# Two attention and scan layers on one core: another order of VectorE and ScalarE work around TensorE

## The chip, the cores and the metric

The kernel runs on one core of a Trainium2 chip, in one launch. The metric is the device time of that core in microseconds (us). The engines are TensorE (PE in the rows; its weight loads are PEld), VectorE (DVE), ScalarE (ACT), GpSimd (POOL) and SyncE (SP), which here only issues the loads of weight tiles. Each engine works through its own program in order; engines wait for each other by semaphores.

## The reference

All tensors are float32. A first block (two layers with feed-forward parts, a pooling mixer and a dilated attention, 512 tokens of width 1024) gives `x`. A second block runs two more layers, and the change lies in these alone. Cut to what matters, one of them is

```python
h  = x  * (1 + scale)   + shift          # 512 latent tokens
hc = cx * (1 + scale_c) + shift_c        # 256 context tokens
(a_q, a_i, a_ff, a_fb, b_q, b_k, b_v, c_q, c_k, c_v, d_q, d_k, d_v, g_lat) = split(h @ w_in)
y_a = hgrn2(a_q, a_i, a_ff, a_fb, ...)                # gated linear scan, forward and backward
y_b = global_gqa(rope(rms(b_q)), rope(rms(b_k)), b_v) # softmax attention, latents and context
y_c = rms(diff_attention(rope(c_q), rope(c_k), c_v, lam))
y_d = window_gqa(rope(d_q), rope(d_k), d_v, sink)     # |i - j| <= 128, plus context, plus a sink
y   = concat(y_a, y_b, y_c, y_d) * silu(g_lat)
x   = layer_norm(alpha * x + gate * (y @ w_out))
```

The scan takes `f = lb + (1 - lb) * sigmoid(z)` as its forget gate, and sums of `log f` over 128 tokens, in both directions. The first of the two layers computes the context's outputs too; the second needs the 512 latents alone.

## The kernel before, in words

**Projections.** A weight tile (1024 x 128) is loaded, rounded by ScalarE to a high part (`hi`, L944), the rest is taken by GpSimd (`remainder`, L843), and TensorE multiplies high and low parts in three passes (`mm3`, L1320). In the two mixer layers a tile is cut into four *quarters* of two 128-row chunks each, so that other work fits between them. Behind the last quarter VectorE takes the result from PSUM (`fill_take`), and a `finish` step ends what the tile needs: head norm, transposed values (L1763, then a copy on VectorE, L2422), rotation (`fill_end`, L2440 to L2444). ScalarE's step behind a quarter of part 3 rounds the tile after the next and, for gates, runs a Silu between two table loads.

**Attention.** There are six attentions a layer (global, diff, window, two head pairs each). For attention `a`, `scores` (TensorE, L1788) are computed in units; VectorE copies each from PSUM and takes its row maximum (L2473), ScalarE exponentiates and sums it (L1227). When all units are done, `rows` makes one number a row out of maxima and sums: a chain of small steps between VectorE (L2495 to L2513) and ScalarE (L1237, L1239), then TensorE transposes (L1799) and ScalarE copies the row (L1241). Then come groups of keys: `weights` (TensorE, L1815) are the transposed scores with the row's number added, ScalarE exponentiates them (L1250), `values` (L1836) sums them into the output. `scores` of attention `a + 1` and `weights` of attention `a` share PSUM banks 2 and 3, so each waits until the other's banks have been read. `end` scales the output by the gate (L2525; diff attentions have a norm first: ScalarE's square L1258, TensorE's L1846, ScalarE's L1261) and splits it in a high and a low part (L1937, L1938).

**The scan.** Per head pair and direction, `sums` makes the sums of log f from the projected gate: a softplus on ScalarE (`nsp`, L989 and L990; two of them in the second layer), VectorE's steps L2314 to L2342 with six scans (L2330), and an Exp on ScalarE (L1154) that waits until VectorE has given `sums_ready`. Then six chunks go through `dist` (GpSimd), `decay` (ScalarE), `operands` (VectorE, L2267 and L2270), `products` (TensorE, L1681), `take` (VectorE, L2281 to L2289), `step` (TensorE, L1698) and `update` (VectorE).

**What sets the order.** `mixer_steps(layer)` writes one list of steps by hand, and every engine walks through it and does what it has in a step. Quarters, score units and groups are dealt out evenly; scan steps are queued in `ticks` and taken one at a time by `tick()`. In the list before the change `rows` stands for all of the chain, and `sums` has three stages: 0 (first softplus' input), 1 (its use, and the second softplus' input), 2 (all that is left, and the Exp).

## Time and profile before

| | us |
|---|---|
| median of 3 runs (lowest, highest) | 3629.45 (3626.37, 3630.61) |
| the profiled execution's own time | 3632.27 |
| its span, first to last instruction | 3630.3 |
| TensorE busy | 3244.4 |
| VectorE, ScalarE, GpSimd busy | 1747.4, 1146.8, 1216.3 |

TensorE works in most of the span; its matmuls are pipelined and their ends are modelled, so busy is not the same as at its peak. The first block lasts to about 2160 us; the first mixer layer and what ends it lie in 2160 to 2960 us, the second in 2960 to 3630 us. The clock granted to TensorE has two levels here, 1.2 and 2.4 GHz, and rows give its mean as a share of the higher.

### The profile page before, as it was taken

The page shows a single profiled execution, that of the slowest core. Times are in us where ns is not written, and L with a number is a line of the kernel's source. Part 1 is how long each engine was busy: PE and PEld are TensorE (multiplying, and loading weights), DVE is VectorE, ACT ScalarE, POOL GpSimd, SP SyncE. Part 2 cuts the span into 40 slices and gives each one's busy share as a digit, 9 for nine tenths or more (in the row PEclk, how much of TensorE's full clock was granted, in tenths as well). Part 3 has the DMA queues.
Part 4 walks back from the last instruction along what each step waited for, and adds up shares of the span by engine and source line. Part 5 has one row for each costly group of instructions (what it writes and reads, how often), then busy time and mean ns, then how long its engine had stood idle before and what let it go on. Part 6 is the DMA issues. An engine that isn't in the chain of part 4 may idle for free.

```text
span 3630.3 us, 53848 instructions
## 1 busy us (share of the span) xinstructions
PE 3244.4 (89%) x20644; PEld 2434.3 (67%) x20644; DVE 1747.4 (48%) x3135; ACT 1146.8 (32%) x1963; POOL 1216.3 (34%) x998
## 2 busy tenths in 40 slices
PE   7999889999899998998899988788979878688787
PEld 5888668777678776776678766555756655455454
DVE  4343765334634364444524366553653266554534
ACT  3222333212422132112312233443434234444343
POOL 3444444444344432222344444311331233213211
PEclk9999999999999999999999989988989988898889
DMA  3222222433233321111233321000101111001011
GB/s 134 93 98 97 77 82 82 139 122 110 100 126 107 133 81 64 53 59 47 81 133 110 122 105 36 25 19 24 36 14 64 47 53 36 30 25 36 24 53 41
DMA packets 74356, 264.66 MB, mean 73 GB/s; under 512 B 7856, under 2 KB 9136, under 8 KB 73904
## 3 DMA queue, kind: packets, MB, share of 16 engines
q1 hardware_dynamic: 67104, 242.25, 19.4%
q10 hardware_dynamic: 7056, 19.69, 1.5%
q8 instruction: 137, 2.24, 0.3%
q14 instruction: 59, 0.48, 0.0%
HBM read 252.47 MB, written 7.34 MB: 72 GB/s over the span
## 4 chain that ended last, share of the span: by engine, by line
PE 71%; DVE 15%; issue 7%; ACT 4%; POOL 2%; DMA 0%; ACTq 0%; DVEq 0%; POOLq 0%
PE ps L1320 53%; PE ps L1815 2%; PE ps L1836 2%; PE ps L1788 2%; POOL wl L855 1%; PE ps L1398 1%; DVE work L2071 1%; DVE tb L2473 1%; PE ps L1681 1%; DVE tb L2118 1%; PE ps L1623 1%; PE ps L1379 1%; PE ps L1641 1%; DVE hc L1984 1%; PE ps L1701 1%
## 5 line engine op out<-in xcount | busy, mean ns | idle before, releaser
L855 POOL TENSOR_TENSOR wl<-raw,wh 128x1024 fp32r<-128x1024 f32 x320 | 791.8, 2474 | 1220.6 <-ACT wh L966 705.4
L1320 PE MATMUL ps<-xh,wh 128*128 128x512 f32 x2400 | 916.2, 406 | 97.5 <-POOL wl L843 30.9
L1320 PE MATMUL ps<-xl,wh 128*128 128x512 f32 x2400 | 864.5, 385 | 0.0
L1320 PE MATMUL ps<-xh,wl 128*128 128x512 f32 x2400 | 862.8, 384 | 0.0
L1320 PEld LDWEIGHTS ps<-xh,wh 128*128 128x128 f32 x2400 | 442.8, 196 | 277.9 <-issue 155.5
L966 ACT ACTIVATE wh<-raw 128x1024 fp32r<-128x1024 f32 x224 | 237.6, 1061 | 982.4 <-PE ps L1320 934.0
L843 POOL TENSOR_TENSOR wl<-raw,wh 128x1024 fp32r<-128x1024 f32 x90 | 220.3, 2448 | 918.0 <-ACT wh L944 918.0
L1320 PEld LDWEIGHTS ps<-xl,wh 128*128 128x128 f32 x2400 | 443.1, 196 | 93.3 <-issue 13.1
L1320 PEld LDWEIGHTS ps<-xh,wl 128*128 128x128 f32 x2400 | 441.2, 195 | 87.6
L1320 PE MATMUL ps<-ah,wh 128*128 128x512 f32 x1104 | 437.5, 403 | 25.4 <-issue 14.2
L1320 PE MATMUL ps<-al,wh 128*128 128x512 f32 x1104 | 420.5, 388 | 0.0
L1320 PE MATMUL ps<-ah,wl 128*128 128x512 f32 x1104 | 420.3, 388 | 0.0
L944 ACT ACTIVATE wh<-raw 128x1024 fp32r<-128x1024 f32 x186 | 196.4, 1057 | 546.9 <-PE ps L1320 496.7
L1227 ACT ACTIVATE tb<-tb,work 128x256 f32<-128x256 f32 (+2 forms) x288 | 165.8, 576 | 385.0 <-DVE work L2479 185.8
L1320 PEld LDWEIGHTS ps<-ah,wh 128*128 128x128 f32 x1104 | 205.6, 189 | 106.6 <-issue 51.2
L2473 DVE TENSOR_SCALAR_CACHE_REDUCE tb<-ps 128x256 f32<-128x256 f32 (+2 forms) x288 | 135.3, 518 | 262.1 <-PE ps L1788 192.8
L2071 DVE TENSOR_TENSOR work<-work 128x512 f32<-128x512 f32 x88 | 245.2, 2786 | 0.0
L1320 PEld LDWEIGHTS ps<-ah,wl 128*128 128x128 f32 x1104 | 205.4, 189 | 43.1
L1320 PEld LDWEIGHTS ps<-al,wh 128*128 128x128 f32 x1104 | 206.0, 190 | 40.2 <-issue 2.0
L2067 DVE TENSOR_TENSOR work<-ps,rs 128x512 f32<-128x512 f32 x66 | 45.7, 692 | 300.2 <-PE ps L1320 300.1
L876 POOL TENSOR_TENSOR hc<-hc 128x64 f32<-128x64 f32 x280 | 95.7, 342 | 169.2 <-PE ps L1686 145.1
L1836 PE MATMUL ps<-work 128*64 128x512 f32 (+2 forms) x448 | 124.3, 636 | 21.0 <-issue 14.1
(348 smaller groups left out, 3625.3 us busy)
## 6 DMA issues: line engine op xcount, KB each, us to landing
raw<-wts_dram SPq DMA_DIRECT2D x458, 512.0 KB, 3.4
spilled_dram<-hc ACTq DMA_DIRECT2D x1, 3072.0 KB, 8.7
hc<-spilled_dram ACTq DMA_DIRECT2D x1, 3072.0 KB, 12.8
tb<-tab_dram ACTq DMA_DIRECT2D x5, 512.0 KB, 3.7
hc<-x_dram ACTq DMA_DIRECT2D x8, 256.0 KB, 9.2
spilled_dram<-hc ACTq DMA_DIRECT2D x1, 2048.0 KB, 7.2
hc<-spilled_dram ACTq DMA_DIRECT2D x1, 2048.0 KB, 9.3
out_dram<-hc SPq DMA_DIRECT2D x8, 256.0 KB, 2.1
```

The costliest lines, as they stand in the source:

```text
L843: pool.tensor_tensor(wl[:, n % SPLIT, :], raw[:, LOADED[n] % RAW, :], wh[:, n % SPLIT, :].bitcast(F32), ALU.subtract).then_inc(lo_done, 1)
L855: pool.tensor_tensor(wl[:, n % SPLIT, :], raw[:, LOADED[n] % RAW, :], wh[:, n % SPLIT, :].bitcast(F32), ALU.subtract).then_inc(lo_done, 1)
L876: pool.tensor_tensor(z[way], border, k_, ALU.subtract)
L944: act.activation(wh[:, n % SPLIT, :], raw[:, at % RAW, :], ACT.Copy).then_inc(hi_done, 1)
L966: act.activation(wh[:, n % SPLIT, :], raw[:, at % RAW, :], ACT.Copy).then_inc(hi_done, 1)
L1227: ins = act.activation(b, b, ACT.Exp, bias=m[:, lane, t:t + 1], scale=scale, accum_out=d[:, lane, t:t + 1])
L1320: ins = pe.matmul(out_, w[:, s, k * P:(k + 1) * P], x_(k, at), start=first, stop=last)
L1788: ins = pe.matmul(ps[:, score_bank(a) + lane, col_:col_ + n], x_[r0:r0 + w, q_tile * P:(q_tile + 1) * P], y_[r0:r0 + w, tok:tok + n], star ...
L1815: ins = pe.matmul(outs[lane], stat, mov, start=number == 0, stop=number == 3 and not g["masks"], skip_group_check=True)
L1836: pe.matmul(flat[HEAD * h:HEAD * (h + 1), g["q0"]:g["q0"] + g["n"]], vv, pring[t % len(pring)][:, 0:g["n"]], start=g["first"], stop=g["las ...
L2071: dve.tensor_tensor(tt[:, j, :], tt[:, j, :], sil[:, j, :], ALU.mult).then_inc(dve_own, 1)
L2473: ins = dve.tensor_scalar(scores_copy[:, lane, col_:col_ + n], ps[:, score_bank(a) + lane, col_:col_ + n], 1.0, -3e38, ALU.mult, ALU.max, ...
```

## The change

No instruction's work changes; what changes is where steps stand in the list, and with it the order in each engine's program.

- `sums` has the stages `abs`, `logs`, `more` (second layer), `scan`, `rest` (backward direction), `keys` and `exp`. The last is ScalarE's Exp, in a step of its own at least one step behind `keys`. `extra_tick` takes sum steps at more places.
- `rows` is split. `math` is the chain on VectorE and ScalarE and stands close behind the last score unit; `rows` is left with the transposes and the copy of the row, behind the last `values`.
- `end` no longer splits the output; `y` does, behind the first `values` of the next attention. `square` (diff) stands behind the last `values`.
- `round` is ScalarE's and GpSimd's rounding with what follows it on ScalarE (Silu, head square). In the groups it stands behind the next `weights`.
- `rope` is the rotation, split from `finish`. `table_in`, VectorE's wait for the rotation tables, stands ahead of the last quarter of the tile that needs it, no longer ahead of the first.
- In a group with several score units the first now stands ahead of the first quarter, and the first `weights` of the next attention stands behind the tail quarter.
- The diff attentions' scaled values get a semaphore of their own (`nlv_ready`).

```diff
@@ def scan_ticks
-        ticks += [[("sums", w, stage)] for stage in range(3)]
+        long = [["scan"], ["rest", "keys"]] if way else [["scan", "keys"]]
+        stages = [["abs"], ["logs"], *([["more"]] if layer else []), *long, ["exp"]]
+        ticks += [[("sums", w, stage) for stage in together] for together in stages]
+        ticks[-2].append(("dist", w, 0))
...
@@ def mixer_steps
     def scores(a, u):
+        if u == 0:
+            flush(ropes)
         steps.extend([("scores", a, u), ("exps", a, u)])
+        if a and u == units[a] - 1:
+            maths.append(("math", a))
+        flush(ropes)
...
-    def quarter(f, part):
+    def quarter(f, part, later=False):
...
         steps.append(("quarter", f, part))
+        if part == 3:
+            rounds.append(("round", f))
+            if not later:
+                flush(rounds)
...
     def finishes():
-        steps.extend(ends)
+        if ends:
+            flush(rounds)
+        for _, f in ends:
+            steps.append(("finish", f))
+            if f[0] in "qk":
+                ropes.append(("rope", f))
...
+    def extra_tick():
+        if ticks and ticks[0][0][0] == "sums":
+            tick()
...
         for i in range(n):
+            if i == 0:
+                finishes()
             if i + 1 < n:
                 steps.append(("weights", a, i + 1))
+            flush(rounds)
             finishes()
+            flush(maths)
             if i == n - 1 and not last:
                 for q in fill[i]:
                     quarter(*q)
                 finishes()
-                steps.append(("rows", a + 1))
                 fill[i] = []
             steps.append(("values", a, i))
+            if i == n - 1:
+                steps.append(("square", a))
+            if i == 0 and a:
+                steps.append(("y", a - 1))
+            extra_tick()
+            if len(due[i]) > 1:
+                scores(a + 1, due[i].pop(0))
...
+                    quarter(*step, later=True)
                 else:
+                    flush(maths)
                     tick()
+                    flush(ropes)
...
+        flush(ropes)
+        if not last:
+            steps.append(("rows", a + 1))
         if a in (1, 3):
             finishes()
             tick(len(ticks))
+        quarter(*tail, later=True)
         if not last:
             steps.append(("weights", a + 1, 0))
-        quarter(*tail)
+        flush(rounds)
         steps.append(("end", a))
...
@@ ScalarE, def sums
-                else:
+                elif stage == "exp":
                     act.wait_ge(sums_ready, w + 1)
...
@@ ScalarE, def mixers
+                def square_(a):
+                    if ATTENDS[a][0] == "diff":
+                        n_q = out_tiles(layer) * P
+                        act.wait_ge(v_used, c.at("item"))
+                        act.activation(osq[:, 0:n_q], banks(0, n_q), ACT.Square).then_inc(osq_ready, 1)
...
@@ VectorE, def mixers
+                def mixed(a):
+                    kind, hp = ATTENDS[a]
+                    n_q = out_tiles(layer) * P
+                    t = sg2[:, 0:n_q]
                     y = 2 * ["scan", "global", "diff", "window"].index(kind) + hp
                     split(t, ahk(y, TOK)[:, 0:n_q], alk(y, TOK)[:, 0:n_q], a_ready, "a")
```

Three places show how this moves instructions. Line numbers are those of each kernel, so a step has another number behind the change.

The first is on ScalarE in the second mixer layer, at the backward sums of the first head pair. Before: the rounding of a tile, a Silu between two table loads, the exponentials of a score unit, the second softplus, the load of the tables, the sums' Exp (L1154), the exponentials of a group's weights (L1250).

```order
L944 ACTIVATE wh<-raw 128x1024
L1198 ACT_TABLE_LOAD
L1198 ACTIVATE hc<-hc 128x512
L971 ACT_TABLE_LOAD
L1227 ACTIVATE tb,work<-tb,work 128x256 x4
L989 ACTIVATE hc<-hc 128x768
L990 ACTIVATE hc<-hc,sm 128x768
L1218 DMA tb<-tab_dram 128x1024
L1154 ACTIVATE work<-work,sm 128x768
L1250 ACTIVATE work<-ps 128x512 x2
```

Behind the change the same stretch reads:

```order
L1277 ACTIVATE tb,work<-tb,work 128x256 x4
L1045 ACTIVATE hc<-hc 128x768
L1046 ACTIVATE hc<-hc,sm 128x768
L1268 DMA tb<-tab_dram 128x1024
L1303 ACTIVATE work<-ps 128x512 x2
L1000 ACTIVATE wh<-raw 128x1024
L1248 ACT_TABLE_LOAD
L1248 ACTIVATE hc<-hc 128x512
L1027 ACT_TABLE_LOAD
L1277 ACTIVATE tb,work<-tb,work 128x512 x2
L1206 ACTIVATE work<-work,sm 128x768
```

The weights' exponentials (now L1303) have passed the rounding, the Silu and the sums' Exp (now L1206), which stands behind one more score unit; the two softplus pairs are still ahead of them.

The second is on TensorE in the first mixer layer, at the sixth group of the second attention. Before: a score unit (L1788), the group's weights (L1815) and values (L1836), then the next quarter (L1320).

```order
L1788 MATMUL ps<-ex,ah 128x256 x4
L1788 MATMUL ps<-ex,al 128x256 x2
L1815 MATMUL ps<-ex,ah 128x512 x2
L1815 MATMUL ps<-ex,al 128x512 x2
L1815 MATMUL ps<-ex,ah 128x512 x2
L1815 MATMUL ps<-lrow,ones_r 128x512 x2
L1836 MATMUL ps<-work 64x512 x2
L1320 MATMUL ps<-xh,wh 128x512
```

Behind the change (scores L1845, quarter L1377, weights L1872, values L1895):

```order
L1845 MATMUL ps<-ex,ah 128x256 x4
L1845 MATMUL ps<-ex,al 128x256 x2
L1377 MATMUL ps<-xh,wh 128x512
...
L1377 MATMUL ps<-xh,wl 128x256
L1872 MATMUL ps<-ex,ah 128x512 x2
L1872 MATMUL ps<-ex,al 128x512 x2
L1872 MATMUL ps<-ex,ah 128x512 x2
L1872 MATMUL ps<-lrow,ones_r 128x512 x2
L1895 MATMUL ps<-work 64x512 x2
```

A whole quarter of twelve matmuls now stands between the last score unit and the weights that use the same banks.

The third is on VectorE in the first mixer layer, ahead of the fourth attention. Before: the rotation of key tile k4 (L2440 to L2444), then the chain of the row statistics (L2495 to L2513).

```order
L2440 TENSOR_TENSOR work<-work,tb 128x512
L2441 TENSOR_TENSOR work<-work 128x512
L2442 CAST ex<-work 128x512
L2444 TENSOR_TENSOR ex<-work,ex 128x512
L2495 TENSOR_TENSOR work<-work 128x16
L2502 TENSOR_TENSOR work<-work 128x16
L2503 TENSOR_TENSOR work<-work 128x16
L2507 TENSOR_TENSOR work<-work 128x24
L2508 TENSOR_SCALAR work<-work 128x24
L2509 CAST hcol<-work 128x24
L2512 COPY work<-hcol 128x24
L2513 TENSOR_TENSOR work<-work,hcol 128x24
```

Behind the change:

```order
L2560 TENSOR_TENSOR work<-work 128x16
L2567 TENSOR_TENSOR work<-work 128x16
L2568 TENSOR_TENSOR work<-work 128x16
L2572 TENSOR_TENSOR work<-work 128x24
L2573 TENSOR_SCALAR work<-work 128x24
L2574 CAST hcol<-work 128x24
L2577 COPY work<-hcol 128x24
L2578 TENSOR_TENSOR work<-work,hcol 128x24
L2470 CAST ex<-ps 128x256
L2471 TENSOR_TENSOR ex<-ps,ex 128x256
L2472 STREAM_SHUFFLE work<-ps 128x512
L2473 TENSOR_TENSOR work<-ps,tb 128x512
```

The chain now stands ahead of the rotation and of the take of k4 from PSUM (L2470 to L2473) as well.

## Rows read from the trace of the kernel before

**Rows 1.** Busy us by engine, granted clock, DMA, in the two mixer layers.

```profile
2160.00:2960.00 800.00, 672.64 (x6534) 482.31 (x6534) 409.32 (x1146) 313.66 (x692) 210.18 (x385) 0.91 0.10 37
2960.00:3600.00 640.00, 520.70 (x4502) 349.50 (x4501) 326.75 (x902) 260.52 (x569) 160.12 (x264) 0.88 0.11 37
```

**Rows 2.** TensorE's waits, 2160 to 3600 us: total us, times, longest.

```profile
PE ps L1788 <- ACT work L1250: 39.2, 13, 15.7
PE ps L1799 <- DVE work L2513: 30.8, 10, 8.8
PE ps L1698 <- DVE work L2289: 24.0, 17, 6.9
...
PE ps L1815 <- issue: 17.6, 9, 4.9
PE ps L1836 <- issue: 14.1, 6, 3.7
...
PE ps L1681 <- DVE hc L2270: 11.8, 11, 2.2
PE ps L1815 <- ACT work L1250: 9.9, 5, 5.4
...
PE ps L1846 <- ACT work L1258: 8.9, 4, 3.3
PE ps L1763 <- DVEq L2526: 8.6, 6, 2.0
```

**Rows 3.** The chain that ended last: two quarters of twelve matmuls (start, us).

```profile
2264.81 3.62 PE ps L1320 x12
2290.77 2.30 PE ps L1320 x12
```

**Rows 4.** Timeline, second layer's backward sums: start, us, engine, line [idle before <-releaser].

```profile
3112.77 0.96 DVE L2325 SCALAR_TENSOR_TENSOR hc<-hc 128x768 f32<-128x768 f32 x1 [4.59 <-DMA tb<-tab_dram]
...
3120.26 0.93 ACT L1154 ACTIVATE work<-work,sm 128x768 f32<-128x768 f32 x1 [10.24 <-DVEq L2344]
3121.10 1.06 ACT L1250 ACTIVATE work<-ps 128x512 f32<-128x512 f32 x2
3122.21 0.80 PE L1788 MATMUL ps<-ah,ex 64*128 64x512 f32 x2 [15.70 <-ACT work L1250]
```

**Rows 5.** Timeline of TensorE: scores behind weights' exponentials that a Silu delays.

```profile
3420.75 0.80 PE L1788 MATMUL ps<-ex,ah 64*128 64x256 f32 x4 [5.96 <-ACT work L1250]
```

**Rows 6.** Timeline of TensorE at the group of the second order excerpt.

```profile
2426.93 0.28 PE L1788 MATMUL ps<-ex,al 32*128 32x256 f32 x2
2432.09 0.80 PE L1815 MATMUL ps<-ex,ah 64*128 64x512 f32 x2 [4.87 <-issue]
```

**Rows 7.** Timeline of VectorE: first and last step of one chain of row statistics.

```profile
2469.14 0.18 DVE L2495 TENSOR_TENSOR work<-work 128x16 f32<-128x16 f32 x1
...
2472.89 0.19 DVE L2513 TENSOR_TENSOR work<-work,hcol 128x24 f32<-128x24 f32 x1
```

**Rows 8.** Timeline of VectorE: the split at the end of the second attention.

```profile
2484.19 1.63 DVE L1937 CAST ah<-work 128x768 fp32r<-128x768 f32 x1
2485.85 0.96 DVE L1938 TENSOR_TENSOR al<-work,ah 128x768 fp32r<-128x768 f32 x1
```

**Rows 9.** Timelines at the second layer's start: take of q0, end of sums, head norm.

```profile
2990.60 0.68 DVE L2405 COPY work<-ps 128x512 f32<-128x512 f32 x1
...
3000.12 0.17 DVE L2342 MEMSET hc<- 128x128 f32 x1
...
2994.14 2.05 PE L1769 MATMUL ps<-work,cn 128*128 128x512 f32 x2 [5.42 <-ACT work L1169]
```

**Rows 10.** Timelines: one rotation's cast, alone and beside GpSimd's remainder.

```profile
2384.33 0.43 DVE L2442 CAST ex<-work 128x512 fp32r<-128x512 f32 x1
...
2729.55 2.91 POOL L843 TENSOR_TENSOR wl<-raw,wh 128x1024 fp32r<-128x1024 f32 x1 [27.35 <-ACT wh L944]
2730.24 2.50 DVE L2442 CAST ex<-work 128x512 fp32r<-128x512 f32 x1
```

More of the change, by code:

```diff
@@ L380, in mixer_steps, with flush @@
 def mixer_steps(layer):
-    steps, ends, ticks = [], [], []
+    steps, ends, ropes, rounds, maths, ticks = [], [], [], [], [], []
     def scores(a, u):
+        if u == 0:
+            flush(ropes)
         steps.extend([("scores", a, u), ("exps", a, u)])
-    def quarter(f, part):
-        while f[0] == "g" and f[1] in SCANS and part == 3 and ("sums", 4 * layer + 2 * SCANS.index(f[1]) + 1, 0) not in steps:
+        if a and u == units[a] - 1:
+            maths.append(("math", a))
+        flush(ropes)
+    def flush(what):
+        steps.extend(what)
+        what.clear()
+    def quarter(f, part, later=False):
+        while f[0] == "g" and f[1] in SCANS and part == 3 and ("sums", 4 * layer + 2 * SCANS.index(f[1]) + 1, "abs") not in steps:
             finishes()
@@ L432, in mixer_steps @@
         finishes()
+        if number == 0:
+            steps.append(("math", 0))
         tick()
+        flush(ropes)
     steps.append(("rows", 0))
@@ L479, in mixer_steps @@
     finishes()
+    steps.append(("y", len(ATTENDS) - 1))
     return steps
@@ L883, in mixers @@
                         dist(*at)
-                    elif step == "quarter" and at[1] == 3:
+                    elif step == "round":
                         remainder(c.at("tile"))
@@ L1239, in rows @@
                     act.activation(lnd[:, 0:n_i * n_l], den2[:, 0:n_i * n_l], ACT.Ln).then_inc(lnd_ready, 1)
+                def rows(a):
+                    n_i = out_tiles(layer)
                     act.wait_ge(lt_full, c.take("lt") + 1)
@@ L1262, in end @@
                     act.activation(b, b, ACT.Exp, scale=-0.5).then_inc(orms_ready, 1)
-                run_ = dict(quarter=quarter, finish=finish, exps=exps, rows=rows, weights=weights, end=end, decay=decay,
+                run_ = dict(round=round_, finish=finish, exps=exps, math=math_, rows=rows, weights=weights, square=square_, end=end, decay=decay,
                             sums=sums, rms=lambda hp: scan_rms(layer, hp), reload=lambda: reload(layer), table=table)
@@ L1831, in values @@
                         pe.wait_ge(v_ready, c.at("v"))
+                    if i == 1 and g["m"]:
+                        pe.wait_ge(nlv_ready, c.take("nlv") + 1)
                     for lane, (r0, w, h) in enumerate(g["lanes"]):
@@ L2331, in sums @@
                     own(ins)
-                    if way:
-                        for t in range(NQ):
-                            b = slice(t * P, (t + 1) * P)
-                            ins = dve.scalar_tensor_tensor(sz[:, b], sw[:, b], se[:, (t + 1) * P - 1:(t + 1) * P], se[:, b], ALU.add, ALU.subtract)
-                        own(ins)
+                elif stage == "rest":
+                    for t in range(NQ):
+                        b = slice(t * P, (t + 1) * P)
+                        ins = dve.scalar_tensor_tensor(sz[:, b], sw[:, b], se[:, (t + 1) * P - 1:(t + 1) * P], se[:, b], ALU.add, ALU.subtract)
+                    own(ins)
+                elif stage == "keys":
                     if layer:
@@ L2526, in end @@
                     dve.sem_inc(o_free, 1)
+                def mixed(a):
+                    kind, hp = ATTENDS[a]
+                    n_q = out_tiles(layer) * P
+                    t = sg2[:, 0:n_q]
                     y = 2 * ["scan", "global", "diff", "window"].index(kind) + hp
                     split(t, ahk(y, TOK)[:, 0:n_q], alk(y, TOK)[:, 0:n_q], a_ready, "a")
-                run_ = dict(quarter=quarter, finish=finish, scores=scores, rows=rows, end=end, table=table, operands=operands, take=take, update=update,
+                run_ = dict(quarter=quarter, finish=finish, rope=lambda f: rope(f[1], f[0]), scores=scores, math=math_, end=end, y=mixed, table_in=table, operands=operands, take=take, update=update,
                             sums=sums, rms=lambda hp: scan_rms(layer, hp), turn=lambda hp: turn(layer, hp), out=lambda hp: scan_end(layer, hp))
```

57 lines of the change are left out of this document (31 added, 26 removed).

## The prediction

> **What bounds the kernel now.** I read first the busy time by stretch [rows 1]. The change lies in 2160 to 3600 us. There TensorE is busy 672.64 of 800 and 520.70 of 640 us; VectorE, the next fullest, has 482.31 and 349.50. So TensorE sets the time, and it stands still for 127.4 + 119.3 = 246.7 us. Its granted clock is 0.91 and 0.88 of the higher level, so (1 − 0.91)·800 + (1 − 0.88)·640 = 149 us of full-rate work are lost to the lower one. The chain that ended last shows what the level does to a step: one quarter takes 3.62 at one place and 2.30 at another [rows 3].
>
> Second, TensorE's waits [rows 2]. Nine kinds lie within the change's reach, together 39.2 + 30.8 + 24.0 + 17.6 + 14.1 + 11.8 + 9.9 + 8.9 + 8.6 = 164.9 us. "Issue" against weights and values means that the profile found no releaser; the timeline tells which bank or exponential it was. No other engine is full, so each wait means that an engine came late to a step, which an order can change.
>
> Third, the timelines at the longest waits, for what stood ahead of the late step.
>
> **The change part by part** (minus is a gain; the sum is made against the profiled execution's own 3632.27).
>
> *a) Scores and weights behind ScalarE's queue* (39.2 + 9.9 = 49.1 in 18 waits). The longest is 15.70 [rows 4]: ScalarE sits in the sums' Exp, idle 10.24, because VectorE is still at the sums and had itself lost 4.59 to the rotation tables' DMA. The weights' exponentials stand behind that Exp, and the scores behind them. Another wait of 5.96 is behind a Silu with its table loads [rows 5]. Read one by one, seven of the 18 are of these two sorts, together 41.5; the others (7.6) stay. The change puts the weights' exponentials ahead of rounding, Silu and Exp, and the tables' wait off that chain. Not all goes: about 3.6 at the longest stays, as VectorE's own sums, some 9 us from 3112.77 to the Exp at 3120.26 with the wait taken off, now delay a copy of scores instead, less what a quarter hides; and 6 in the second layer, where two softplus pairs still stand ahead of the weights (first order excerpt). −41.5 + 9.6 = **−32**, bounds −41.5 and −20.
>
> *b) Row statistics* (30.8 in ten waits [rows 2]). The transposes wait for a chain that takes 2472.89 + 0.19 − 2469.14 = 3.9 us [rows 7], with ScalarE's two small exponentials and a logarithm inside. `math` starts it behind the last score unit, ahead of a group's last work, so the transposes should find it done. But the chain now stands ahead of the rotation and of the take from PSUM on VectorE (third excerpt), and the engine is held through its waits. The chain is 1.6 longer than the quarter of 2.3 that may cover it, and with the take behind it what follows comes 2 to 4 us late; at about six places another step needs that take soon. I take back 6 × 2.5 = 15: **−16**, bounds −30.8 and 0.
>
> *c) Weights behind VectorE's copy* (17.6 in nine). At the second excerpt's place the scores end at 2427.2 and the weights that share their bank start at 2432.09, after 4.87 [rows 6]; until then VectorE copies the scores out. The change puts a quarter between them, 2.30 of other work at the higher clock. That and the finer dealing should cover 12 of the 17.6; the copy itself takes no less. 2.30 times nine is 20.7, so all of it could go. The next scores then wait a little for the weights, about 6 in all: **−12**, bounds −17.6 and −4.
>
> *d) Ends* (values 14.1, square's 8.9, finish behind VectorE 8.6: 31.6). The split, 1.63 + 0.96 = 2.6 us [rows 8], leaves VectorE's end at ten places, and the square of the diff attentions starts behind the last values. Against that, the first weights now stand behind the tail quarter and the next ones directly behind them, so values meet exponentials of 1.06 [rows 4] at some eight places (8.5), and `lrow`'s copy in the second layer may stand behind two softplus. About 18 goes and 8 comes: **−10**, bounds −26 and 0.
>
> *e) The scan* (24.0 behind take, 11.8 behind operands). Nothing makes it shorter. A step and the next products stand directly together at three more places, where the longest wait is 2.2 [rows 2]; the turn of each head pair waits a little less. **+4**, bounds 0 and +6.6.
>
> *f) Start of a layer.* Before, VectorE takes q0 at 2990.60, ahead of the sums, which end at 3000.12 [rows 9]. Behind the change scan and keys stand ahead of it, so q0's head norm, for which TensorE waits 5.42 already, comes up to 7.7 later; quarters of other tiles stand between and hide most of it. **+2** a layer, +4, bounds 0 and +15.
>
> *Rounding behind the exponentials*, with GpSimd's remainder behind it, costs nothing by itself: a rounded tile is used two tiles (eight quarters, over 18 us) later. Its instructions stay the same and pass no DMA queue that is late. Loads of weight tiles depend on the raw buffer's release, a group later at most. But where it falls matters to VectorE: a cast that takes 0.43 alone takes 2.50 beside a remainder of 2.91, and ends 0.3 behind it [rows 10]. The sum takes this at nothing, since such meetings happen before too (that row is one) and the change moves them rather than makes them.
>
> *g) The clock.* With fewer gaps more of the time should be at the higher level. Between nothing and a quarter of the 149, 37 us; the gain so far is a quarter of the 247 idle, but part of the low stretches stands at waits which stay (e). I take **−12**.
>
> *h) What stood behind.* A wait removed lets TensorE reach the next late step sooner, and VectorE and ScalarE still have to do the same work in order. A quarter of a to d, 70/4: **+17**, bounds 0 and +35.
>
> Sum: −32 − 16 − 12 − 10 + 4 + 4 − 12 + 17 = −57, so 3632.3 − 57 = 3575. The median of the runs lies 2.8 under the profiled execution: **3572 us**, 1.6% faster.
>
> **The rivals.**
>
> *A, the forecast*, 3545 to 3600.
>
> *B, VectorE's hold gives most of it back.* The math chain with its waits on ScalarE stands ahead of takes and scores' copies, and TensorE waits there instead of at the transposes. For it: 3.9 against a quarter's 2.3. Against it: VectorE is busy only 60% and 55% of the mixers. Then b and d give nothing, c −6, a −32, e and f +8, h a quarter of 38, and no clock: −20.5, 3609.
>
> *C, the waits go as listed.* No step takes back: −41.5 − 30.8 − 17.6 − 26 = −116, a quarter of it met later (+29), e and f +8, and the clock −18: −97, 3532. For it: the waits are at separate places and most chains are shorter than two quarters. Against it: the weights and scores that alternate on two banks, a loop that no order opens.
>
> *D, no measurable change.* Less than 0.2% (7.3 us), about what a measurement of this kernel can tell, needs B and 15 us more lost, say f at its bound.
>
> *E, slower: GpSimd's remainders meet VectorE's steps.* `round` now stands behind the weights and their exponentials, in which VectorE does takes, rotations and copies that TensorE waits for. A meeting costs 2.50 − 0.43 = 2.1 us [rows 10]. The mixers have 76 roundings (38 tiles a layer); with the forecast's gain of 57 it decides from 57/2.1 = 27 more of them that hit a step on the path. With 45, +95 − 57 = +38: 3667. For it: remainder starts follow the rounding directly, and VectorE is busy more than half of the time. Against it: before, roundings stood behind a quarter, just where VectorE takes the tile, so that they met it there as well.
> The Trainium skill, page "SBUF — State Buffer", section "SBUF: two separate sides", says that VectorE and GpSimd share a pair of ports as an exclusive lock that is held for a whole instruction, the loser being fully blocked, so by it every such meeting would cost the rest of the remainder, at most 2.9 a time. The cast of [rows 10], which ends just behind the remainder, agrees. By that rule alone, with each of the 76 roundings blocking a step on the path to its end, the sum would be −57 + 76 × 2.1 = +103.
>
> **How the numbers follow.** A 0.55, B 0.15, C 0.15, D 0.06, E 0.09. The likeliest is A, 3572. The range reaches from beyond C (3520, for a clock that gives all of its 37: 3532 less a part of the 19 above its −18) to what is faster by 0.2% (3622), which holds B; D and E, 0.15, stay out. Faster by over 0.2%: A, B, C, 0.85; within: 0.06; slower: E, 0.09.
>
> **What would show it.** a is right if scores' waits behind weights' exponentials fall from 39.2 to under 15 and none of 15.70 is left; b if the transposes' 30.8 falls below 10 while takes and scores' copies gain no more than some 15 us of wait; c if the weights' "issue" wait falls to about 6. d shows in values, square and finish: 31.6 to about 20. e: waits behind take and operands rise from 35.8 to about 40. f: q0's head norm waits longer than 5.42. g: the granted clock of the mixers rises by about 0.01. E would show as VectorE's mean times of takes, casts and copies rising with the same work, and its busy time above 832. The prediction is wrong if TensorE waits as long in the mixers as before at other lines (B, h), or if idle time falls and the span doesn't because the clock falls.

## The result, and the profile after

The median went from 3627.91 (four runs, three of them in the table above) to 3602.87 us: ratio 0.9928, 95% interval 0.9911 to 0.9946, so 25 us or 0.7% faster. The forecast was 3572, 57 us faster: the sign and the range hold it, the size is less than half.

The busy time of the two mixer layers after the change [rows 1]. Behind the window and its length stand TensorE's matmuls, its weight loads, VectorE, ScalarE and GpSimd, then the granted clock:

```profile
2160.00:2960.00 800.00, 683.25 (x6625) 492.81 (x6623) 424.99 (x1157) 321.47 (x703) 215.31 (x389) 0.91 0.11 40
2960.00:3600.00 640.00, 524.68 (x4490) 347.61 (x4488) 335.69 (x926) 262.90 (x578) 149.16 (x260) 0.88 0.10 35
```

More is done in the same time, but the granted clock is 0.91 and 0.88 as before. TensorE's waits in the same stretch [rows 2] (step is now L1755, products L1738, scores L1845, weights L1872, values L1895, the transposes of `rows` L1856, of a values' tile L1820, the head norm L1826; behind the arrow VectorE's take L2348, operands L2329, chain L2578, end L2591, ScalarE's weights' exponentials L1303):

```profile
PE ps L1755 <- DVE work L2348: 44.8, 32, 7.4
PE ps L1377 <- issue: 28.1, 17, 6.2
PE ps L1738 <- DVE hc L2329: 20.4, 9, 8.5
PE ps L1872 <- issue: 17.9, 7, 6.1
PE ps L1820 <- DVEq L2591: 17.8, 6, 4.4
PE ps L1826 <- ACT work L1221: 16.2, 2, 11.2
...
PE ps L1845 <- ACT work L1303: 10.8, 17, 2.7
...
PE ps L1856 <- DVE work L2578: 3.6, 2, 2.5
...
PE ps L1872 <- ACT work L1303: 2.5, 2, 1.3
```

Scores and weights behind the exponentials fell from 49.1 to 13.3, the transposes' wait from 30.8 to 3.6: the two waits that the change aimed at are gone. But the scan's two waits rose from 35.8 to 65.2, the weights behind a copy stayed at 17.9, the finish rose from 8.6 to 17.8.

Where the 15.70 was [rows 4], ScalarE now does the weights' exponentials behind the second softplus, then rounding, table load and Silu; the scores wait 2.67 there:

```profile
3092.55 0.93 ACT L1046 ACTIVATE hc<-hc,sm 128x768 f32<-128x768 f32 x1
...
3093.39 1.06 ACT L1303 ACTIVATE work<-ps 128x512 f32<-128x512 f32 x2
3094.34 1.06 ACT L1000 ACTIVATE wh<-raw 128x1024 fp32r<-128x1024 f32 x1
3095.42 1.28 ACT L1248 ACT_TABLE_LOAD   x1
```

```profile
3094.51 0.50 PE L1845 MATMUL ps<-ah,ex 64*128 64x512 f32 x2 [2.67 <-ACT work L1303]
```

Two places show what the early chain of row statistics [rows 7] costs. The first layer, ahead of the fourth attention, VectorE:

```profile
2621.62 0.20 DVE L2560 TENSOR_TENSOR work<-work 128x16 f32<-128x16 f32 x1
2623.97 2.42 DVE L2567 TENSOR_TENSOR work<-work 128x16 f32<-128x16 f32 x1 [2.15 <-ACT work L1287]
...
2627.68 0.19 DVE L2578 TENSOR_TENSOR work<-work,hcol 128x24 f32<-128x24 f32 x1
...
2629.20 0.67 DVE L2473 TENSOR_TENSOR work<-ps,tb 128x512 f32<-128x512 f32 x1
```

and TensorE beside it:

```profile
2629.98 0.98 PE L1377 MATMUL ps<-xh,wh 128*128 128x512 f32 x2 [6.23 <-issue]
```

The chain takes 6.2 here; for 2.15 of it VectorE stands still for ScalarE, and 2.42 is one step that mostly takes 0.17 (last section). Behind it is the take of a projected tile from PSUM (L2470 to L2473), and the next quarter starts when that take ends, 6.23 late: it writes the bank that was taken. The profile names no releaser, but the wait goes with the chain: the longest of its kind is 2.2 before the change and 2.5 with the chain put back (e2, below).

At the second layer's start the chain of the first attention stands between a head norm (which waits 3.96 for ScalarE) and the scan's update and operands; the products wait 8.54, of which the chain itself is 2.5:

```profile
3032.55 0.75 DVE L2493 SCALAR_TENSOR_TENSOR work<-work,pr,ps 128x512 f32<-128x512 f32 x1 [3.96 <-ACT ps L1228]
...
3034.79 0.17 DVE L2560 TENSOR_TENSOR work<-work 128x8 f32<-128x8 f32 x1
...
3037.21 0.57 DVE L2363 SCALAR_TENSOR_TENSOR hc<-hc,sm,ps 64x64 f32<-64x64 f32 x2
3037.82 0.29 DVE L2326 TENSOR_TENSOR hc<-hc,work 128x128 f32<-128x128 f32 x1
```

```profile
3039.11 0.36 PE L1738 MATMUL ps<-work 64*32 64x32 f32 x16 [8.54 <-DVE hc L2329]
```

And the same layer's first head norm [rows 9] waits 11.24, 5.42 before: VectorE takes q0 at 2985.07, behind the sums.

```profile
2986.63 2.04 PE L1826 MATMUL ps<-work,cn 128*128 128x512 f32 x2 [11.24 <-ACT work L1221]
```

The weights behind a copy are late for another reason than before. VectorE is at the backward sums (9.5 us in one go, from 2316.98 on), with the score unit's copy behind them:

```profile
2316.98 0.96 DVE L2376 SCALAR_TENSOR_TENSOR hc<-hc 128x768 f32<-128x768 f32 x1
...
2318.97 4.16 DVE L2389 TENSOR_TENSOR_SCAN hc<-cn,hc 128x128 f32<-128x128 f32 x6
...
2326.69 0.69 DVE L2538 TENSOR_SCALAR_CACHE_REDUCE tb<-ps 128x512 f32<-128x512 f32 x1 [0.23 <-DVE hc L2402]
```

```profile
2328.10 0.79 PE L1872 MATMUL ps<-ah 64*128 64x512 f32 x2 [6.12 <-issue]
```

One kind of wait can take over another's; the sum of all is TensorE's idle time, the span less its busy time. Before, it is 3630.3 − 3244.4 = 385.9 us. The page of the profiled execution after the change says

```profile
span 3603.6 us, 53856 instructions
...
PE 3243.4 (90%) x20644; PEld 2433.5 (68%) x20644; DVE 1745.8 (48%) x3135; ACT 1144.1 (32%) x1963; POOL 1206.9 (33%) x998
```

which is 360.2 idle, with as many matmuls as before. So this execution is 26.7 shorter by 25.7 of idle and 1.0 of busy time. Idle times below are worked out in the same way, from one execution of each kernel.

### The profile page after: what moved, and what is told of

Its sections match the earlier page's. It is cut to its first block, busy times and chain, and to the rows that moved or that the text cites. A ratio compares the mean times of both kernels' runs of the same rounds, so it can differ in the third digit from the quotient of the medians.

```text
span 3603.6 us, 53856 instructions
## 1 busy us (share of the span) xinstructions
PE 3243.4 (90%) x20644; PEld 2433.5 (68%) x20644; DVE 1745.8 (48%) x3135; ACT 1144.1 (32%) x1963; POOL 1206.9 (33%) x998
## 4 chain that ended last, share of the span: by engine, by line
PE 71%; DVE 15%; issue 7%; ACT 4%; POOL 2%; DMA 0%; ACTq 0%; DVEq 0%; POOLq 0%
PE ps L1377 53%; PE ps L1872 2%; PE ps L1895 2%; PE ps L1845 2%; POOL wl L911 1%; DVE tb L2538 1%; DVE work L2130 1%; PE ps L1738 1%; ACT tb L1277 1%; DVE tb L2177 1%; PE ps L1680 1%; DVE hc L2043 1%; PE ps L1455 1%; DVE work L2341 1%; PE ps L1436 1%
## 5 line engine op out<-in xcount | busy, mean ns | idle before, releaser
L1377 PE MATMUL ps<-xh,wh 128*128 128x512 f32 x2400 | 910.7, 404 | 97.4 <-POOL wl L899 30.7
L1377 PE MATMUL ps<-xl,wh 128*128 128x512 f32 x2400 | 860.2, 383 | 0.0
L1377 PE MATMUL ps<-xh,wl 128*128 128x512 f32 x2400 | 859.0, 382 | 0.0
L1377 PEld LDWEIGHTS ps<-xh,wh 128*128 128x128 f32 x2400 | 441.4, 195 | 261.3 <-issue 142.7
L1377 PEld LDWEIGHTS ps<-xl,wh 128*128 128x128 f32 x2400 | 439.6, 194 | 93.0 <-issue 13.2
L1377 PEld LDWEIGHTS ps<-xh,wl 128*128 128x128 f32 x2400 | 437.9, 193 | 87.4
L1377 PE MATMUL ps<-ah,wh 128*128 128x512 f32 x1104 | 440.6, 406 | 28.7 <-issue 17.5
L1377 PE MATMUL ps<-al,wh 128*128 128x512 f32 x1104 | 423.0, 390 | 0.0
L1377 PE MATMUL ps<-ah,wl 128*128 128x512 f32 x1104 | 421.6, 389 | 0.0
L1377 PEld LDWEIGHTS ps<-ah,wh 128*128 128x128 f32 x1104 | 207.1, 191 | 110.4 <-issue 54.5
L1377 PEld LDWEIGHTS ps<-ah,wl 128*128 128x128 f32 x1104 | 207.0, 191 | 44.1
L1377 PEld LDWEIGHTS ps<-al,wh 128*128 128x128 f32 x1104 | 207.4, 191 | 41.1 <-issue 2.0
L1303 ACT ACTIVATE work<-ps 128x512 f32<-128x512 f32 (+2 forms) x224 | 108.7, 536 | 202.9 <-PE ps L1872 159.0
```

What stands on the lines that cost most here:

```text
L1303: act.activation(pring[t % len(pring)][:, 0:g["n"]], ps[:, weight_bank(a, i, lane), 0:g["n"]], ACT.Exp, scale=scale).then_inc(exp_done, 1)
L1377: ins = pe.matmul(out_, w[:, s, k * P:(k + 1) * P], x_(k, at), start=first, stop=last)
```

## The experiments

Each ratio is to the kernel before on the same chip; its interval is 0.0009 to 0.0019 to each side, 3 to 7 us, so two kernels that differ by less than some 8 us are not told apart. Differences in us are differences of ratios times 3630. Expectations speak of theories: 1, that too little of TensorE's work stands between a chunk's products and its step; 2, that the chain holds VectorE ahead of the scan; 3, that a score unit's copy does.

### Why the scan waits longer

**Empty scan steps** (e1_phase).

```diff
+        if w in (2, 3, 5, 6):
+            ticks.append([("idle", w)])
```

> The changed kernel with one empty scan step put behind the sums' Exp of four directions (third, fourth, sixth and seventh), so that a chunk's products and its step stand a group apart again (weights, values, quarter, scores between them) instead of one quarter. Theory 1, spacing: TensorE waits 46.0 for takes and 20.4 for operands only because 2.4 us of other work stand between products and step, while copy and take need 4; both together fall from 66 to about 35, and the time falls by 20 to 30 to about 3575 to 3583. Theory 2, VectorE held: row statistics and sums stand ahead of the takes wherever they lie, the two waits together stay above 55, and the time stays within 7 of 3603.

Ratio 0.9936 [0.9918, 0.9954], 3 us behind the changed kernel and not told apart from it. The waits of products and step changed places:

```profile
PE ps L1740 <- DVE hc L2331: 44.3, 19, 8.6
...
PE ps L1757 <- DVE work L2350: 21.8, 16, 7.4
```

The sum is 66.1, against 65.2. Theory 1 fell: VectorE's work is late on whichever side of the quarter it is due.

**Quarter first** (e4_quarter_first).

```diff
-            if len(due[i]) > 1:
-                scores(a + 1, due[i].pop(0))
```

> The changed kernel without the score unit ahead of a group's first quarter; the units stand behind the quarters, as before the change. If the early score unit is what delays the takes (its copy stands ahead of them on VectorE), the step's 46 falls by 15 or more and the time falls by 10 to 15. If the spacing of products and step is the cause, most of which this leaves at one quarter, the step's wait falls by 3 to 8 at the fifth and last chunks alone, the weights behind a copy gain as much, and the time stays within 7 of 3603.

0.9934 [0.9919, 0.9949], not told apart from the changed kernel. The step's wait fell from 44.8 to 37.8, the weights' behind a copy rose from 17.9 to 34.4. So the early unit earns its waits at the weights and pays a good part at the scan.

**Scan step ahead of the unit** (f2_scan_first).

```diff
-                if number % 2 == 0 and due[i]:
+                if (number % 2 or len(between) == 1) and due[i]:
                     scores(a + 1, due[i].pop(0))
```

> The changed kernel with the score unit between two scan steps put behind the first of them, so that VectorE takes the chunk ahead of the unit's copy and TensorE has a score unit and a quarter (3.3) between products and step. Theory 3 (the copy ahead of the take): waits of step and products fall from 66 to 30 to 42 and the time by 15 to 25 to about 3578 to 3588. Theory 2 (VectorE held by chain and sums): they fall by less than 12, and the time stays within 10 of 3603, or rises, since the units' exponentials come later.

0.9906 [0.9891, 0.9921], 8 faster than the changed kernel, at the edge of what is told apart. No theory is met: step and products wait 50.5, 14.7 less, where theory 3 has 30 to 42 and theory 2 a fall of less than 12. The copy is late for the weights now:

```profile
PE ps L1872 <- issue: 50.5, 25, 5.5
PE ps L1738 <- DVE hc L2329: 25.4, 10, 8.5
PE ps L1755 <- DVE work L2348: 25.1, 17, 7.4
```

TensorE's idle time did not fall by this edit: 363.0 against 360.2.

**Chain behind the scan step** (f1_math_behind).

```diff
-                    flush(maths)
                     tick()
+                    flush(maths)
                     flush(ropes)
...
         quarter(*beside.pop(0))
+        tick()
         finishes()
         if number == 0:
             steps.append(("math", 0))
-        tick()
```

> The changed kernel with the chain of row statistics one place later: behind the scan step that it now stands ahead of, and at the start of a layer behind the scan step with the head norm too. Theory 2 (the chain holds VectorE ahead of the scan): waits of step and products fall from 66 by 10 to 18 (the 8.5 at the second layer's start nearly goes), the transposes stay under 8, and the time falls by 8 to 14 to about 3590 to 3595. Theory 3 (the copy of the score unit that is computed just ahead of the scan step stands ahead of take and update): the two waits fall by less than 8 and the time stays within 6 of 3603.

0.9906 [0.9889, 0.9922], 8 faster, again at the edge. Step and products wait 36.5 and 13.5 (15.2 less), the longest at products 2.1 in place of 8.5, and the transposes 7.3. The waits are as theory 2 has them, with two limits. At a layer's start the head norm's finish moved behind the scan step as well, and the second layer's start makes 6.9 of the 15.2, so that part is not the chain's alone. And idle time fell by 3.0 only, to 357.2: quarters wait 4.7 more and the transposes 3.7.

### What each part is worth

**Chain back** (e2_math): `math` directly ahead of `rows` in the changed list.

```diff
-            maths.append(("math", a))
...
-            steps.append(("rows", a + 1))
+            steps.extend([("math", a + 1), ("rows", a + 1)])
```

> The changed kernel with the chain of row statistics put back directly ahead of the transposes, nothing else undone. Theory 1, spacing: the step's wait for takes stays at 46 within 5; the transposes wait some 27 again, and the time rises by 15 to 27 to about 3618 to 3630. Theory 2, VectorE held by the chain: the waits of step and products fall by 20 or more, which pays for most of the transposes' 27, and the time stays within 7 of 3603.

0.9974 [0.9961, 0.9986], 17 slower. The time is theory 1's, but the step's wait fell from 44.8 to 36.8, where theory 1 has it stay; step and products together fell by 9.3, less than half of theory 2's 20. The transposes wait more than before the change, where `rows` stood ahead of the last values; here it stands behind them, and the chain with it:

```profile
PE ps L1854 <- DVE work L2576: 49.2, 11, 12.7
```

So this is not the price of the old place; for that the old list is needed. The next kernels take the list of before and change one part of it. They share one thing more that no run tries alone: the diff values' own semaphore.

**Early chain alone** (p2_math_alone). In the old list:

```diff
+        if a and u == units[a] - 1:
+            maths.append(("math", a))
...
                 else:
+                    flush(maths)
                     tick()
```

> The order before the change with one part alone: the chain of row statistics close behind the last score unit, ahead of the next scan step; all else as before. If the chain's hold of VectorE costs the scan as much alone as in company, the transposes' 30.6 falls to under 8, the waits of step and products rise from 35 by 8 to 15, and the kernel is 12 to 20 faster than the one before. If it costs nothing alone, it is 24 to 30 faster. If the transposes' place was hidden by a later wait, within 7.

1.0012 [1.0002, 1.0022]: 4 us *slower*. The transposes' wait went from 30.8 to 7.2, and what it gave stands elsewhere:

```profile
PE ps L1346 <- issue: 28.0, 17, 8.2
PE ps L1724 <- DVE work L2317: 26.6, 17, 6.9
PE ps L1707 <- DVE hc L2298: 20.7, 14, 4.7
...
PE ps L1825 <- DVE work L2547: 7.2, 4, 4.2
```

Quarters +7.5, step +2.6, products +8.9, and the products' second form (behind L2293) from 1.8 to 5.0: 22 of the 23.6. The 8.2 is the bank's wait of above, at the same attention; ahead of the take stand the chain (4.0) and two steps of the sums, one of which took 2.98 beside a remainder on GpSimd. So not all of this wait is the chain's. The idle time says the same of the whole, 3644.4 − 3258.0 = 386.4 against 385.9 before:

```profile
span 3644.4 us, 53856 instructions
...
PE 3258.0 (89%) x20644; PEld 2444.2 (67%) x20644; DVE 1749.5 (48%) x3135; ACT 1146.9 (31%) x1963; POOL 1215.4 (33%) x998
```

**Chain behind the scan step, alone** (p4_math_behind_alone): as p2, with `flush(maths)` behind `tick()`.

> The order before the change with the early chain of row statistics alone, but behind the next scan step, not ahead of it. Theory 2 (the chain pays what it saves only because it stands ahead of the scan and of the take): waits of step and products stay within 5 of the 35 before, and it is 10 to 20 faster than the kernel before. If the chain's saving is given back whatever stands behind it (the quarters' bank, the rotation), it stays within 7 of the kernel before.

0.9991 [0.9980, 1.0002], no change that can be measured. The transposes still wait 13.3 and the products 19.3. Theory 2 alone is not enough. Quarters wait 26.3 (20.5 before), so in the old list the chain seems to be in the way of takes too; that is argued, not tried.

**Late roundings and Exp alone** (p1_late_alone). In the old list:

```diff
                     quarter(*step, later=True)
...
                 steps.append(("weights", a, i + 1))
+            flush(rounds)
             finishes()
...
+            ticks.append(([("sums", w, "exp")] if p == 0 else []) + here("dist", p) + ...
```

> The order before the change with one part alone: in the groups each rounding stands behind the next weights, and the sums' Exp stands one scan step later; all else as before. Passed on (the banks that scores and weights share let a wait only change sides): the waits behind the weights' exponentials fall from 48 to under 20, the weights' wait behind the copy rises from 17.6 to 25 or more, and the kernel is 10 to 20 faster than the one before. Worth its waits (it loses only beside the other parts): 28 to 36 faster.

0.9933 [0.9916, 0.9950]: 24 us faster, all that the whole change gives, between the two theories. The 49.1 fell to 9.2 (6.7 and 2.5), the weights behind a copy rose from 17.6 to 30.4 and the transposes from 30.8 to 37.1:

```profile
PE ps L1819 <- DVE work L2541: 37.1, 11, 11.3
PE ps L1835 <- issue: 30.4, 8, 8.9
```

A gain of 40 at one kind of wait, 19 met later at two others.

**Late roundings, Exp in its place** (p6_rounds_alone): p1 without the line on `exp`.

> The order before the change with the late roundings alone, and the sums' Exp left in the step of the keys, where it stood. If the longest waits (15.7 and those like it) are the Exp's, this keeps about half of the 24 that both gave: 8 to 16 faster than the kernel before. If the roundings with the Silu behind them are most of it, because the weights' exponentials pass the Exp as well where a group's weights stand ahead of the flush, 18 to 25 faster.

0.9971 [0.9959, 0.9983], 10.5 faster. The scores still wait 27.6, at most 13.9. So the Exp's step of its own carries about 14 of the 24.

**Roundings and Exp back, in the changed list** (f3_late_undone).

```diff
-            if not later:
-                flush(rounds)
+            flush(rounds)
...
-        long = [["scan"], ["rest", "keys"]] if way else [["scan", "keys"]]
+        long = [["scan"], ["rest", "keys", "exp"]] if way else [["scan", "keys", "exp"]]
```

> The changed kernel with each rounding back directly behind its quarter and the sums' Exp in the step of the keys: the part that took scores and weights from behind ScalarE's queue is undone, the rest stays. If its 36 us of waits were worth their length, the waits behind the weights' exponentials rise from 12 to 40 or more and the time rises by 25 to 36 to about 3630 to 3640. If a quarter or more of them was only passed on to the scan and the copies, the time rises by 10 to 25.

0.9973 [0.9962, 0.9983], 16 slower. The scores wait 43.4 again, the weights behind a copy only 6.4: the two share banks, and one's wait is the other's cover.

**Both parts** (p3_late_math): p1 and p2 together.

> The order before the change with two parts: the late roundings (with the sums' Exp a scan step later) and the early chain of row statistics. If the two just add (late roundings alone gave 24, the early chain alone cost 4), it is 15 to 24 faster than the kernel before. If the chain is worth more once the roundings are late (the transposes then waited 36.9 instead of 30.6, and within the whole change undoing the chain cost 17), it is 32 to 45 faster, and then the other parts of the change lose 10 or more.

0.9934 [0.9921, 0.9948], 24 faster: p1 again. They don't help each other; the chain's place is worth nothing that can be measured beside the late roundings either (idle 365.2, 367.5 in p1).

**Units alone** (p5_units_alone), the old list with the early unit and the weights behind the tail quarter.

```diff
+            if len(due[i]) > 1:
+                scores(a + 1, due[i].pop(0))
...
+        quarter(*tail)
         if not last:
             steps.append(("weights", a + 1, 0))
-        quarter(*tail)
```

> The order before the change with one part alone: the first of several score units ahead of a group's first quarter, and the next attention's first weights behind the tail quarter. By the forecast the weights' 17.6 behind the copy falls to about 6 and the kernel is some 10 faster. If the banks' loop only passes the wait to the scores, which then wait for the weights' exponentials (38.6 before, 48 or more then), or to the scan's takes, it stays within 7.

0.9983 [0.9974, 0.9992], 6 faster. The weights' 17.6 went to 1.5, and 11.4 of it came back at the exponentials:

```profile
PE ps L1809 <- ACT work L1267: 45.8, 19, 16.0
...
PE ps L1836 <- ACT work L1267: 14.7, 8, 5.3
```

**Split back** (f4_y_undone): `("y", a)` directly behind `("end", a)`.

> The changed kernel with the split of an attention's output directly behind its end again. By the forecast's step on the ends the values and the finish wait some 10 us more and the time rises by 8 to 12 to about 3613. If VectorE's place does not matter there, because the values now meet exponentials and not the split, the time stays within 5 of 3603.

0.9923 [0.9910, 0.9936]: no difference to the changed kernel.

**Scan held at the start** (e3_start).

```diff
+        hold = f == ("q", 0) and part < 3 and ticks and ticks[0][0][2:] == ("scan",)
...
+            if not hold:
+                tick()
```

> The changed kernel with the sums' scan and keys held until VectorE has taken q0 from PSUM, at the start of each of the two layers. If the start's loss is as large as its waits say (head norm 16.2 in two waits, 7.5 before), those fall to about 7 and the time falls by 8 to 10 to about 3594. If other work hides it, because the scan then starts some 7 us later and its products wait instead, the time stays within 4 of 3603.

0.9909 [0.9890, 0.9928], 7 faster; the head norm's wait fell from 16.2 to 8.3. This part's size agrees with its waits, but 7 is not told apart from nothing; idle time fell by 4.0.

### A faster version

**Start and chain** (g1_start_math): e3 and f1.

> The changed kernel with two edits together: scan and keys held until q0 is taken, and the chain of row statistics behind the scan step. Each alone gave some 7 to 8; they lie at different places but for the second layer's start, so together 12 to 15 faster than the changed kernel (ratio to before about 0.989). If the start's two edits meet the same wait, 8 to 10.

0.9874 [0.9859, 0.9890], 20 faster than the changed kernel, not told apart from the 15 of the two alone.

**And the scan step first** (g2_start_math_scan): e3, f1 and f2.

> As the run before, and with the score unit behind the first of two scan steps. If that unit's place only trades waits of the scan against waits of the weights, as it did alone (takes 46 to 26, weights 18 to 50), this is within 7 of the run before. If the trade pays since the chain no longer stands ahead of the takes, it is 8 or more faster still (ratio to before 0.987 or less).

0.9859 [0.9842, 0.9876]: by this ratio 51 us faster than before (the medians are 3581.52 and 3636.55), the lowest ratio of all. Over g1 it is 5, not told apart.

```profile
PE ps L1874 <- issue: 49.6, 25, 5.5
...
PE ps L1757 <- DVE work L2350: 22.7, 17, 4.9
...
PE ps L1740 <- DVE hc L2331: 15.2, 9, 3.9
```

The scan's waits are at 37.9, near the 35.8 of before, and the weights wait for the copies instead. The profiled execution is 55.2 shorter than the one before the change: 37.1 of idle time, and 18.1 because the same matmuls took less, at a granted clock of 0.950 in place of 0.943.

**Finish as before** (g3_all): g2 with the finish behind the attention's second weights.

> The best run so far (scan held until q0 is taken, chain behind the scan step, score unit behind the first of two scan steps) with the finish of a tile behind an attention's second weights again, as before the change. The finish waits 17.8 for VectorE's end there and 8.6 before; if that is on the path, it is 6 to 10 faster than that run (ratio to before about 0.983 to 0.984). If the weights in front of it wait for the same banks, within 4 of it.

0.9877 [0.9862, 0.9892]: not faster than g2, 6 slower if anything (not told apart). The finish's wait fell from 17.8 to 10.1; values (7.5) and weights (7.8, 2.5 in g2) took it over.

**Sums behind the copies** (g5_scan_not_extra): g2, and `extra_tick` leaves `scan` and `rest` alone.

> The best run so far (scan held until q0 is taken, chain behind the scan step, score unit behind the first of two scan steps), with the sums' long VectorE steps (six scans, and the backward direction's six more) taken at the ordinary places only, behind a score unit's copy, not at the extra ones ahead of it. The weights' longest waits of 6.1 and 3.3 stood behind such a step. If they go and nothing takes their place, 4 to 9 faster than that run (ratio to before about 0.984); if the later sums delay the scan by as much, within 4 of it.

0.9862 [0.9847, 0.9877], as g2. The weights' wait fell from 49.6 to 43.5, without an effect that the times show.

## Why the prediction was too large

**a, right.** 49.1 fell to 13.3, none over 2.7 among the scores. Alone it gave 24: the forecast's −32 with its own quarter of h taken back is −24. It was put down to seven waits behind Silu and Exp; p6 splits it into 10 for the roundings and 14 for the Exp. (VectorE's sums behind the tables' DMA take 7.5 by the rows that the forecast gives, not 9.)

**b is the step that failed.** "I take back 6 × 2.5 = 15: −16" should have taken back all. The transposes' wait went as forecast (3.6, under 10), and the time did not: +4 alone ahead of the scan step, −3 behind it, nothing beside a. Alone, it left TensorE's idle time where it was (386.4, 385.9). What the forecast named for it (the chain with its waits stands ahead of takes and copies) is what happened, and at up to 8.5 a place, not 2.5: the bank of a quarter (6.23), the products at the second layer's start (8.54, with the head norm's part in it). Rival B was the right story, and it was set aside with VectorE's mean share of 60% and 55%. Those are TensorE's weight loads, the column beside it in [rows 1]; VectorE's 409.32 of 800 and 326.75 of 640 us are 51% in both layers. Yet no such share is an argument: the chain blocks an in-order engine while that engine idles (2.15 inside the chain, 3.96 ahead of it), and what is queued behind it is what TensorE waits for next.

**c, half.** Alone 6 of the 12, since the scores then wait for the exponentials. In the whole change 17.9 is left: with a, the weights come sooner (30.4 in p1), and the sums' extra places put up to 9.5 of VectorE's work ahead of a copy.

**d.** The kinds of wait fell as a sum (values, square and finish, 31.6 before; the finish alone 17.8 after, which meets the forecast's sign), but the split's place is worth nothing, and the finish's place only trades waits. No −10 was found. The square's move was not tried by itself.

**e, mis-sized.** Forecast 40, measured 65.2. It isn't the scan's own order (e1): it is b's chain, with the head norm's finish at a layer's start (15.2 of it, f1), and c's early unit (some 9, e4), counted nowhere in their terms.

**f.** Forecast +4, measured +7 (e3), not told apart from it.

**g, open.** "I take −12": in the same windows the granted clock is 0.91 and 0.88 in both kernels. Over the same work, from VectorE's first take of a tile (2165.59 and 2172.53) to the end, it is 0.89 and 0.90, and TensorE is busy 1207.59 and 1199.65, 7.9 less. But in the same two executions the stretch ahead, which did not change, took 7.0 more (last section), so this pair can't settle it. Nor does the clock simply follow the idle time: f2 has 2.8 more of it than the changed kernel, and the layers' matmuls took 7.7 less there.

**h.** +17 was too little for b and about right for a.

From the parts: a −24, b 0, c −6, f +7 make −23; measured −25. With their intervals the sum is known to some 12 us, and f was priced in the changed list, so this only says that d and the rest did nothing large. By idle time the parts are −18.4 (p1), +0.5 (p2), −8.5 (p5) and +4.0 (e3), together −22.4 of the −25.7.

**E did not come.** VectorE is busy 1745.8 in the whole kernel (1747.4 before; the forecast's 832 for the layers is the weight loads' column again, VectorE's was 736), and the rotation's cast that took 2.50 beside a remainder [rows 10] has a longest of 459 ns:

```profile
L2507 DVE CAST ah<-work x12: 426/427/459, 2190.7 to 3306.9; 128x512 fp32r<-128x512 f32 x12
L2507 DVE CAST ex<-work x8: 426/427/427, 2267.9 to 3422.8; 128x512 fp32r<-128x512 f32 x8
```

## What to carry to other kernels

A wait that an order removes is worth what it says only if the step that is moved ahead does not stand, on its own engine, in front of what the waiting engine needs next; a chain that hops between two engines holds the first for its whole length, whatever its mean load. Price a part by making it alone in the old order: undoing it in the new one priced a place that never existed (17 us against nothing). Where two kinds of work share banks, add up both waits: here 39.2, 9.9 and 17.6 were one sum, 66.7. In the old list what left it was about the time gained: 27 and 24 us with the late roundings and Exp, 10 and 10.5 with the roundings, 5 and 6 with the units. In the changed list, where the scan's waits move too, it is not so: f2 adds 27 to this sum and is not slower.

## What the runs showed of the hardware

A VectorE step in the chain with a median of 0.17 us took 2.42 at one place, beside GpSimd's `dist`, a run of steps of 0.3 us each from 2619.82 to 2627.3:

```profile
L2567 DVE TENSOR_TENSOR work<-work x12: 166/167/2422, 2270.1 to 3512.6; 128x8 f32<-128x8 f32 x8, 128x16 f32<-128x16 f32 x4
```

```profile
2624.09 0.35 POOL L932 TENSOR_TENSOR hc<-hc 128x64 f32<-128x64 f32 x1
```

It outlasted eight of them or so, while the chain's steps of the same form just ahead of it and behind it, beside the same run, took 0.20 and 0.21. So a tiny step on the path was slow beside a string of small GpSimd steps, as a larger one was beside one long one [rows 10]. The Trainium skill, page "SBUF — State Buffer", section "SBUF: two separate sides", has the loser of the two blocked for a whole instruction of the other, which as an estimate from these rows would be 0.3. What made it 2.42 wasn't tried, and that GpSimd did is not shown.

The stretch ahead of the two layers, which the change leaves alone, ended 7 us later in the profiled execution after the change than in the one before:

```profile
2149.60 0.87 DVE L1953 TENSOR_SCALAR work<-hc,ada 128x512 f32<-128x512 f32 x2
```

```profile
2156.56 0.87 DVE L2012 TENSOR_SCALAR work<-hc,ada 128x512 f32<-128x512 f32 x2
```

So the two profiled mixers differ by 34 us where the medians differ by 25; a single profile of this kernel is good for places, not for the last 7 us. The 7 us are not waits: up to VectorE's first take of a tile in the layers, at 2165.59 and 2172.53, TensorE is idle 128.8 and 128.7 us and busy 2036.80 and 2043.79, with the same 9577 matmuls, at a granted clock of 0.98 and 0.97. Other kernels' profiles have the shorter stretch (g2: 2165.58) or the longer one (p2: 2172.34), so it goes with the execution and not with the change. Why the clock fell is open.
